# Expert weights on two queues: up weights issued by SP after the up projection, down weights by ACT after the rows are evicted

## What is computed

```
combine = jnp.sum(jax.nn.one_hot(eid, N_EXPERTS) * gate[..., None], axis=1)
hg = jnp.einsum('nd,edf->nef', x, w_eg)
hu = jnp.einsum('nd,edf->nef', x, w_eu)
hidden = jax.nn.silu(hg) * hu * combine[..., None]
return jnp.einsum('nef,efd->nd', hidden, w_ed)
```

## Time and profile before

| | before |
|---|---|
| median of 3 runs | 1852.25 us (1850.18 to 1853.36) |
| the profiled execution's own time | 1860.25 us |
| its span | 1858.3 us |
| mean granted TensorE clock in it | 0.848 |
| PE busy | 1385.5 us (75%) |
| DVE, ACT, POOL busy | 830.8, 336.5, 291.3 us |
| DMA moved | 268.77 MB |
| queue q1 (SP), q0 (POOL), q10 (ACT) | 157.25, 107.06, 3.27 MB |

### The profile page before, as it was taken

How to read it: one execution, slowest core, us unless ns; L and a number is a source line. 1 busy time by engine, 2 the same in 40 slices (tenths; PEclk the granted TensorE clock), 3 DMA queues, 4 the chain that set the end, 5 groups by cost and what they waited for, 6 DMA issues and landing times. The chain is left out here.

```text
span 1858.3 us, 18772 instructions
## 1 busy us (share of the span) xinstructions
PE 1385.5 (75%) x7353; PEld 792.4 (43%) x7353; DVE 830.8 (45%) x1566; ACT 336.5 (18%) x776; POOL 291.3 (16%) x308
## 2 busy tenths in 40 slices
PE   5799999992499901587767679937988686789960
PEld 5435575551255501342323236736764343344420
DVE  3269999939746996222222223124241111111218
ACT  2520110112343103421211111111111010011110
POOL 2100000010000000033433410000033332333320
PEclk9899999995558955688888889966999997899985
DMA  6402232130000100045665662072108988888803
GB/s 211 176 23 71 63 113 68 46 128 34 0 1 2 44 11 0 12 159 204 221 232 188 227 215 80 23 274 93 57 13 313 366 350 331 327 322 313 319 12 142
DMA packets 87317, 268.77 MB, mean 145 GB/s; under 512 B 16047, under 2 KB 50599, under 8 KB 76663
## 3 DMA queue, kind: packets, MB, share of 16 engines
q1 hardware_dynamic: 50832, 157.25, 22.8%
q0 software_dynamic: 33920, 107.06, 16.3%
q10 hardware_dynamic: 2479, 3.27, 0.6%
HBM read 292.58 MB, written 23.00 MB: 170 GB/s over the span
## 5 line engine op out<-in xcount | busy, mean ns | idle before, releaser
L743 PE MATMUL ps<-arena 128*128 128x64 f32 (+3 forms) x1216 | 334.5, 443 | 0.6 <-ACT arena L1170 0.6
L1054 PE MATMUL ps<-arena 128*64 128x256 f32 x1568 | 208.2, 412 | 57.4 <-DMA arena<-in_w_gu,arena 55.6
L743 PEld LDWEIGHTS ps<-arena 128*128 128x128 f32 (+1 forms) x1216 | 187.8, 198 | 147.1 <-issue 147.0
L651 POOL DMA_INDIRECT arena<-in_kv,arena x128 | 121.1, 946 | 686.5 <-ACT arena L1245 297.8
L1054 PEld LDWEIGHTS ps<-arena 128*64 128x64 f32 x1568 | 115.6, 148 | 145.2 <-DMA arena<-in_w_gu,arena 65.9
L749 PE MATMUL ps<-arena 128*128 128x256 f32 (+5 forms) x640 | 133.3, 374 | 1.5 <-ACT arena L1226 1.5
L1515 DVE SCALAR_TENSOR_TENSOR arena<-arena 128x512 f32<-128x512 f32 (+1 forms) x232 | 120.3, 518 | 8.3
L749 PEld LDWEIGHTS ps<-arena 128*128 128x128 f32 (+1 forms) x640 | 111.2, 201 | 23.3 <-issue 4.6
L1120 ACT ACTIVATE arena<-ps 128x256 f32<-128x256 f32 (+5 forms) x148 | 61.1, 417 | 278.5 <-PE ps L914 67.2
L1741 DVE COPY arena<-ps 128x128 f32<-128x128 f32 x49 | 14.3, 291 | 201.5 <-PE ps L1064 193.4
L1079 PE MATMUL ps<-arena 128*64 128x512 f32 x392 | 94.9, 605 | 0.5 <-issue 0.5
(11 more groups left out here) (299 smaller groups left out, 1509.1 us busy)
## 6 DMA issues: line engine op xcount, KB each, us to landing
arena<-in_w_gu SPq DMA_DIRECT2D x32, 2048.0 KB
arena<-in_w_dn SPq DMA_DIRECT2D x32, 1024.0 KB
arena<-in_w_in SPq DMA_DIRECT2D x20, 1024.0 KB, 5.5
arena<-in_w_o SPq DMA_DIRECT2D x4, 1024.0 KB, 5.0
arena<-in_w_pg SPq DMA_DIRECT2D x4, 1024.0 KB, 6.5
arena<-scr_ypair SPq DMA_DIRECT2D x4, 1024.0 KB, 6.5
arena<-in_x_prompt SPq DMA_DIRECT2D x4, 512.0 KB, 9.8
scr_h<-arena SPq DMA_DIRECT2D x4, 512.0 KB, 4.6
```

Of the source, the lines that this page charges most:

```text
L651: pl.indirect_dma_start(kv(g, 2 * j + t), None, I["kv"], bass.IndirectOffsetOnAxis(ap=offs[:, t, n:n + 1], axis=0)).then_inc(kv_in[g % 2 * ...
L743: mm = nc.tensor.matmul(out, w[:, k], hT[:, k, a:b], start=(k == 0), stop=(k == KC - 1))
L1054: mm = nc.tensor.matmul(PS[2 + p % 2][64 * half:64 * half + 64, 0:2 * P], xT[:, p % 3, j, 64 * h:64 * h + 64], w[:, k, half, :], start=(k ...
```

## The change

SP waits for `u_full` of base block e - 3 in place of `y_full`, and then issues only the up weights. The down weights of expert e are issued by ACT, right after `rows_act` of base block e - 3. The first three experts, the overflow weights and everything on the other engines stay.

```diff
             for e in range(3, NE):
-                sp.wait_ge(y_full, POS[("base", e - 3)] + 1)
-                load_expert(e)
+                sp.wait_ge(u_full, POS[("base", e - 3)] + 1)
+                sp.dma_start(eset[e % 3][:, 0:2 * KC * F], I["w_gu"][e * P:(e + 1) * P, :]).then_inc(up_in[e % 3], 16)
...
                 nc.scalar.activation(ys[:, p % YR, :], PS[5 + p % 2][:, :], cp).then_inc(y_act, 1)
+                kind, e = BLOCKS[p]
+                if kind == "base" and e + 3 < NE:
+                    e += 3
+                    act.dma_start(eset[e % 3][:, 2 * KC * F:], I["w_dn"][e * P:(e + 1) * P, :]).then_inc(down_in[e % 3], 16)
```

## The result

| | before | after |
|---|---|---|
| median of the runs | 1853.58 us (6 runs, 1850.18 to 1857.2) | 1961.78 us (6 runs, 1956.66 to 1965.07) |
| ratio, 95% interval | | 1.0573 (1.0557 to 1.059) |
| span of the profiled execution | 1858.3 us | 1962.0 us |
| expert stage, first turn to last down projection | 411.3 us | 520.6 us |

The change costs 108 us. The forecast was 1904 us, 52 more than before, with a range up to 1940: the right sign and about half of the size. The measured time lies beyond the range.

A forecast was written before the change was run, and what follows sets the result against it. PE stops for overflow loads without slack, never for base weights, so delaying those loads delays PE: six real cycles at 3.0 us (18) plus seven empty at 4.9 (34) add 52 to 1852.25, giving 1904 us; range 1862 to 1940.

The forecast's parts named there:

- The moments: From Y, the end of an overflow block's down projection: base up loads -2.5 and +3.9, POOL's gather +2.8, overflow load +4.1 us.
- No slack for POOL's requests: Overflow loads, real or empty, land no earlier than PE wants them, so what delays them delays PE.
- ACT's issues at nothing: 29 DMA issues on ACT, 0.53 us each, covered by its 3.27 us idle before the next sigmoid: 0; uncovered, 15 us.
- Slow matmuls behind each new stop: Up projection after a new stop at an empty load: sixteen matmuls take 3.68 us against 1.90, +1.8 each; forecast +12.6.
- Waits for rows: PE's waits for gathered rows (scr_x) after the second base block go, -1.6 us per empty cycle; forecast -11.
- the empty cycles: Cycles whose overflow load moves no weights: new stop 4.7 us behind the gather, 4.9 net with side effects; 7 x 4.9 = 34 us.
- the real cycles: Cycles whose overflow load moves weights: 7.35 MB at 0.395 MB per us lands 3.0 us later; 6 x 3.0 = 18 us.
- A: Rival: gather and empty load pass between large packets, so only cycles with real loads cost, +18 us: 1870; chance 0.14.
- B: Rival: a third full queue, q10, delays POOL's requests 2 us more per empty cycle, 14 in all: about 1918; chance 0.15.
- The main case: Real overflow loads cost 18 us and empty ones 34, with down weights moved to ACT at 0: 1904 us; chance 0.56.
- C: Rival: the channel carries the same bytes and PE waits for none that move, so nothing changes: 1852; chance 0.08.
- D: Rival: the first up load leaves 8.9 us earlier, gather waits go and overflow loads land earlier: about 1821; chance 0.07.

The follow-up runs named there:

- the run with one overflow down load: The change without the overflow down loads after the first, so later overflow blocks compute with O0's down weights: 1865.32 us against 1764.87 for the kernel before, ratio 1.0575.
- the one-queue run: The change with its down weights issued by SP at `y_full`, so all base weights go on q1: 1851.14 us against 1761.7 for the kernel before, ratio 1.0505.

## Why the prediction was right and wrong

**Right.** *PE never waits for base weights*, before or after, so the change could win nothing at the point it works on. The moments: L592 at Y - 2.4 and Y + 3.9, POOL at Y + 2.9 and Y + 4.3. *No slack for POOL's requests*: what delays them delays PE; the runs that gave them slack turned the cost from 100 us to 13. *ACT's issues at nothing*, as far as ACT's own time goes: the issue stands beside the eviction, and ACT keeps its idle time before the next sigmoid:

```profile
1596.53 0.28 ACT L1335 ACTIVATE arena<-ps 128x128 f32<-128x128 f32 x1 [3.27 <-PE ps L1054]
1598.98 0.60 ACT L1341 ACTIVATE arena<-ps 128x512 f32<-128x512 f32 x1 [2.17 <-PE ps L1079]
1598.99 0.33 ACTq L1345 DMA_DIRECT2D arena<-in_w_dn  x1
```

Slow matmuls behind each new stop (3.68 us for a first half): +14.8 against +12.6. Waits for rows: -14.7 against -11.

**Wrong: the empty cycles, 4.7 us each, measured 9.4** (65.8 / 7). The step was "I take the gather at 8.0 us ... and the empty load behind it at Y + 11.0". The empty load came at Y + 6.3 + 9.4 = Y + 15.7 on average. In the cycle shown above the gather ahead of it was not what held it: q0's small packets of that time were through by 1767 (Y + 6.4), and for the next 2 us q0 had nothing in the channel. (The first of the five empty cycles from 1690 to 1840 us is less clear: there packets of 4 KB ran on, on q0, for 4 us and more after the empty load's issue, and it landed latest, 13.0 us after it. The gather may have had a part in that one.) The empty load waits by itself, until the second up load has run dry and the down load nearly so. This is the upper bound that the text gives: q1 and q10 together have to drain at the lower rate, from Y + 4, 10.9 us, to Y + 14.9. That empty loads are what stops PE is shown by the run without them; that they wait for *both* queues is read from the times only.

**Wrong: the real cycles, 3.0 us each, measured 7.1** (42.5 / 6). Two parts. I took the cycle with a stop of 8.66 us as the pattern, and it is the longest of the six, whose mean is 44.0 / 6 = 7.3: 1.3 us. The rest is the landing: stops of 14.4 us on average put it at Y + 20.7, where the sum gave Y + 18.1. The term that was mis-sized is the rate of 0.395 MB per us for its 7.35 MB. The 0.394 of the real cycle above agrees with it only by luck: it counts the overflow down weights, which the sum left out and which cost nothing by the run with one overflow down load. Without them it was 0.340 and 0.348; at 0.348 the sum gives 21.1 us and Y + 20.6. The overflow load didn't take part from the start: in the first 4.3 us after its request (Y + 4.1 to Y + 8.4) q0 moved 0.07 MB and none of the weights; in the kernel before it moved 0.92 MB in the first 4.3 us, most of it weights. Why its weights come so late behind a queue that is full stays open.

**Wrong: the range.** It ended at 1940 since "the sum of all upper bounds", 1955, was left out; the measured 1962 lies beyond even that. Both terms have one cause, a request of POOL's that meets full queues, and both came out at or above their upper bounds together (7.1 against 6.9, and for the empty cycles a stop of 9.4, where the bound has 14.9 - 6.3 = 8.6). Bounds with a common cause have to be taken together.

**The rivals.** A (only real loads pay) is refuted: empty loads cost more. B (three queues worse than two) was right in direction and too small: on top of the early loads the third queue costs some 20 us, and by itself, with no early load, 51 us, though there at the gathers and not at the empty loads that B has a price for. The main case had this queue in no term: it put the down weights' move to ACT at 0. The Trainium skill says in DMA: Bandwidth & Descriptors, "Issuing engines are not separate DMA queues", that another issuer buys issue time and no bandwidth. No run here gained by it, and the 51 us that down weights by ACT alone cost are a loss that this rule doesn't tell. The turns between queues that the Trainium skill describes in DMA: Bandwidth & Descriptors, "Queues, rings and completion order", agree in direction with the empty up loads, which landed after 8.9 to 11.0 us beside one other queue and 9.9 to 13.0 beside two. C (nothing changes) is refuted. D (faster) is right for one half of it, though not by its own condition: the first early load does shorten the stops, by 20 us in sum; the second makes the stops 125 us longer (55.8 to 180.4).

## What to carry to other kernels

Before moving a load to an earlier moment, look in the waits for the one that an engine is stopped by; an earlier load that nobody waits for is put in front of it. A request has to be costed by what all queues still hold when it goes out, even if it moves next to nothing, and a further full queue counts too. If two requests share a queue and both have no slack, moving one of them only changes which is late; give slack to both at once.

## What was unexpected of the hardware

- An indirect DMA with no row to move still had 144 tiny packets. It landed in 2.1 us on a free channel and in 9.1 to 11.8 us beside two full queues.
- The same bytes, at nearly the same moments, on two queues in place of one made the waits for small gathers grow from 22.5 to 58.7 us.
- Taking the overflow down weights (1 MB) off q0 in a cycle with three full queues brought nothing: the rate up to the landing was 348 in place of 380 GB/s, and the stops stayed (88.3 against 86.5 us).
- The same kernel took 1762 us in one group of runs and 1859 us in another, though the record has chip 8 for both; another chip is thus not shown as the cause, and none is known. The first turn of the expert stage came at about 1300 and 1390 us: the difference lies ahead of that stage. In slices 19 to 22 of the pages, ahead of it, the DMA engines moved 188 to 232 GB/s in the profile before and 324 to 329 in that of the one-queue run.
